# First mixer of a two-layer encoder step: index scores before the value product, forget gates before keys and queries, output-gate units between the level passes

## The reference, cut to what matters

```python
z = u @ w_in
aq, af, ai, ag, bq, bk, bv, bqi, bki, bw = jnp.split(z, split_at, axis=-1)
# gated linear recurrence (A), 4 heads of 128
qa = silu(aq);  ka = (1 - lb) * sigmoid(-af);  va = ai
log_f = logaddexp(log(lb), log1p(-lb) + log_sigmoid(af))     # forget gates
oa, s_fin = hgrn2_recurrence(qa, ka, va, log_f, s0)          # b = cumsum(log_f) in chunks of 64
oa = rms(oa) * o_gain * sigmoid(ag)                          # output gates
# sparse attention (B): index scores, the top keys of each row, then attention over them
q = rope(rms_norm(bq)); k = rope(rms_norm(bk)); qi = rope(bqi); ki = rope(bki)
score = sum_h relu(qi_h @ ki.T) * wi_h                       # wi = bw / 2
ob = attention(q, k, bv, top_k(score))
return concat(oa, ob) @ w_out
```

## Time and profile before

| | us |
|---|---|
| median of 3 runs | 2174.45 (2172.32 to 2175.32) |
| the profiled execution, its own time | 2178.14 |
| its span, first to last instruction | 2176.4 |
| PE busy | 1996.0 (92% of the span) |
| DVE / ACT / POOL busy | 1358.7 / 1111.3 / 778.2 |
| mean granted clock of PE | 0.957 of 2.4 GHz |

### The profile page before, as it was taken

How to read it: one execution, slowest core, us unless ns; L and a number is a source line. 1 busy time by engine, 2 the same in 40 slices (tenths; PEclk the granted TensorE clock), 3 DMA queues, 4 the chain that set the end, 5 groups by cost and what they waited for, 6 DMA issues and landing times. The chain is left out here.

```text
span 2176.4 us, 35434 instructions
## 1 busy us (share of the span) xinstructions
PE 1996.0 (92%) x13900; PEld 1508.1 (69%) x13900; DVE 1358.7 (62%) x2050; ACT 1111.3 (51%) x1334; POOL 778.2 (36%) x446
## 2 busy tenths in 40 slices
PE   4999999999998788979999997999999678999999
PEld 2677777665776655657777775777777456777777
DVE  7777853314987743276787437778743667778632
ACT  5677854112143234057778335777843217778621
POOL 4766500000037402147571014776400426667000
PEclk9999999997998889989999999999999879999999
DMA  3223222210111020012222211332322201322221
GB/s 134 85 93 113 92 100 80 87 49 5 63 59 63 6 87 20 20 39 97 97 97 100 107 66 39 108 104 97 101 99 73 79 3 60 115 97 92 99 105 40
DMA packets 24025, 167.06 MB, mean 77 GB/s; under 512 B 3024, under 2 KB 3024, under 8 KB 8176
## 3 DMA queue, kind: packets, MB, share of 16 engines
q1 hardware_dynamic: 22176, 157.98, 20.9%
q0 software_dynamic: 1744, 7.66, 1.0%
HBM read 161.80 MB, written 3.83 MB: 76 GB/s over the span
## 5 line engine op out<-in xcount | busy, mean ns | idle before, releaser
L1661 PE MATMUL ps<-big 128*128 128x296 f16 x2464 | 717.2, 291 | 39.6 <-ACT big L667 12.4
L1665 PE MATMUL ps<-big 128*128 128x296 f16 x2464 | 716.6, 291 | 13.1 <-DVE big L1013 12.8
L1662 PE MATMUL ps<-big 128*128 128x296 f16 x2464 | 716.9, 291 | 0.0
L1642 PE MATMUL ps<-big 128*128 128x296 f16 x4224 | 540.0, 291 | 10.5 <-DVE big L1113 10.4
L1642 PEld LDWEIGHTS ps<-big 128*128 128x128 f16 x4224 | 411.2, 98 | 133.4 <-DVE big L1113 11.7
L384 POOL TENSOR_TENSOR big<-big 128x512 f32<-128x512 f32 x88 | 123.4, 1402 | 634.5 <-ACT big L558 388.0
L1661 PEld LDWEIGHTS ps<-big 128*128 128x128 f16 x2464 | 242.1, 98 | 119.1 <-issue 16.1
L1665 PEld LDWEIGHTS ps<-big 128*128 128x128 f16 x2464 | 242.2, 98 | 91.1 <-DVE big L1013 20.9
L1636 PE MATMUL ps<-big 128*128 128x296 f32 x992 | 264.6, 429 | 34.3 <-DVE big L1571 25.3
L1662 PEld LDWEIGHTS ps<-big 128*128 128x128 f16 x2464 | 242.4, 98 | 67.7
L1636 PEld LDWEIGHTS ps<-big 128*128 128x128 f32 x992 | 195.2, 198 | 98.8 <-issue 25.4
(11 more groups left out here) (270 smaller groups left out, 2074.2 us busy)
## 6 DMA issues: line engine op xcount, KB each, us to landing
big<-in_w_up SPq DMA_DIRECT2D x88, 1024.0 KB, 4.8
big<-in_w_dn SPq DMA_DIRECT2D x32, 1408.0 KB, 6.0
big<-in_w_in SPq DMA_DIRECT2D x20, 512.0 KB, 3.5
big<-in_w_out SPq DMA_DIRECT2D x1, 4096.0 KB, 12.7
resid<-in_x SPq DMA_DIRECT2D x4, 592.0 KB, 6.6
out_y<-resid SPq DMA_DIRECT2D x8, 296.0 KB, 4.7
big<-in_w_ai POOLq DMA_DIRECT2D x1, 2048.0 KB, 10.1
big<-in_w_pool POOLq DMA_DIRECT2D x1, 1024.0 KB, 5.2
```

Of the source, the lines that this page charges most:

```text
L1642: last = mm(ps[:, bank + hf, 0:HALF], w, x[:, hf * HALF:(hf + 1) * HALF], start=start, stop=stop)
L1661: mm(out, w[:, 0, c], xop[:, 0, x, c], start=start, stop=False, skip_group_check=True)
L1662: mm(out, w[:, 1, c], xop[:, 0, x, c], start=False, stop=False, skip_group_check=True)
L1665: last = mm(out, w[:, 0, c], xop[:, 1, x, c], start=False, stop=(c == DC // 2 - 1), skip_group_check=True)
```

## The change

The units are put in another order, and so are the instructions of PE, ACT, DVE and POOL around them. In `w_in` the forget gates now come before the key: index key 0, index queries 1 and 2, `af` 3 to 6, key 7, queries 8 to 11, `aq` 12 to 15, `ag` 16 to 19. Core of the diff (lines that only move are mostly shown where they arrive):

```diff
+            pool.wait_ge(s["isc_acc"], 4 * TILES)
+            g.memset(att, 0.0).then_inc(s["att_zero"], 1)
+            pool.dma_start(states_hi[:, 2], d["state"]).then_inc(s["state_in"], 16)
             pool.wait_ge(s["gate_l1"], 1)
             link(g.tensor_scalar(gate_b, zf, 0.0, None, ALU.min))
...
+            def proj(n, dst, h, func):
+                act.wait_ge(unit_done, U + n + 1)
+                a.activation(split(dst[:, h]), halves(unit_bank(n)), func).then_inc(s["raw_evac"], 1)
+            for n, dst in enumerate((kit, qit[:, 0], qit[:, 1])):
+                act.wait_ge(unit_done, U + n + 1)
+                a.activation(split(dst), halves(unit_bank(n)), ACT.Copy).then_inc(s["raw_evac"], 1)
...
+            proj(AF, zf, 0, ACT.Copy)
+            for t in range(TILES):
+                act.wait_ge(s["ai_mm"], t + 1)
+                a.activation(va[0:ROWS[t], t], ps[0:ROWS[t], 4 + t % 2, :], ACT.Copy).then_inc(s["ai_evac"], 1)
+            for h in range(1, HEADS):
+                proj(AF + h, zf, h, ACT.Copy)
+            act.wait_ge(s["raw_evac"], 7)
...
+            def query(h):
+                act.wait_ge(unit_done, U + BQ + h + 1)
+                a.activation(split(qt[:, h]), halves(unit_bank(BQ + h)), ACT.Copy, scale=cgain[:, 0:1])
+                if h >= 1:
+                    act.wait_ge(s["ksum_mm" if h == 1 else "qsum_mm"], 1 if h == 1 else h - 1)
+                a.activation(split(square[:, (h + 1) % 2, :]), halves(unit_bank(BQ + h)), ACT.Square) \
+                    .then_inc(s["qk_sq"], 1)
+            proj(BK, kt.rearrange("p (h n) -> p h n", h=1), 0, ACT.Copy)
+            a.activation(split(square[:, 0, :]), halves(unit_bank(BK)), ACT.Square).then_inc(s["qk_sq"], 1)
+            query(0)
             act.wait_ge(s["ksum_mm"], 1)
             a.activation(split(root), halves(6), ACT.Sqrt, bias=eps[:, 0:1], scale=1.0 / DH) \
                 .then_inc(s["kroot_done"], 1)
-            for h in range(HEADS):
-                proj(12 + h, qa, h, ACT.Silu)
+            query(1)
...
-            for h in range(2):
-                proj(16 + h, ag, h, ACT.Sigmoid)
+            for h in range(2, HEADS):
+                query(h)
             for h in range(HEADS):
                 last = a.activation(ka[:, h], ka[:, h], ACT.Exp, bias=lb_ln[:, h:h + 1])
             last.then_inc(s["gate_ka"], 1)
-            for h in range(2, HEADS):
-                proj(16 + h, ag, h, ACT.Sigmoid)
+            act.wait_ge(s["qsum_mm"], 4)
+            a.activation(rqs[:, 0:4], ps[:, 4, 0:16].rearrange("p (t h) -> p t h", t=4), ACT.Sqrt, bias=eps[:, 0:1],
+                         scale=1.0 / DH)
+            a.activation(rqs[0:ROWS[4], 4], ps[0:ROWS[4], 4, 16:20], ACT.Sqrt, bias=eps[0:ROWS[4], 0:1],
+                         scale=1.0 / DH).then_inc(s["qroot_done"], 1)
+            for h in range(HEADS):
+                proj(AQ + h, qa, h, ACT.Silu)
             act.wait_ge(s["scan_done"], 1)
             diffs = 0
             for n, (kind, hp, h) in enumerate(DECAYS):
                 cols = NT if kind != "level" else MAIN if h == 64 else TAIL0 if h >= 16 else NT
                 e = decay[:, n % 2, :, 0:cols]
+                for h in range(HEADS):
+                    if n == GATE_AT[h]:
+                        proj(AG + h, ag, h, ACT.Copy)
...
+            act.wait_ge(s["raw_evac"], 16)
+            a.activation(ag, ag, ACT.Sigmoid).then_inc(s["ag_done"], 1)
...
+                a.activation(kd_tok[0:ROWS[t], t], ps[0:ROWS[t], t % 2, :], ACT.Copy).then_inc(s["kdt_evac"], 1)
...
+            dve.wait_ge(s["gate_logf"], 1)
+            for h in range(HEADS):
+                for lo, w in SEGMENTS:
+                    last = v.tensor_tensor_scan(zf[:, h, lo:lo + w], ones[:, 0:w], zf[:, h, lo:lo + w], 0.0, ALU.mult,
+                                                ALU.add)
+            last.then_inc(s["scan_done"], 1)
             dve.wait_ge(s["k_normed"], 1)
             dve.wait_ge(s["rope_in"], 32)
+            for n in range(5):
+                dve.wait_ge(s["kperm_mm"], n + 1)
+                rope(kt if n == 0 else qt[:, n - 1], 1, rope_bank(n))
+                dve.wait_ge(s["rope_done"], 3 + n + 1)
...
-            for n in range(5):
-                if n == 4:
-                    dve.wait_ge(s["gate_logf"], 1)
...
-            dve.wait_ge(s["raw_evac"], 16)
+            dve.wait_ge(s["raw_evac"], 12)
...
+                        ps[:, 2 + 3 * (n % 2) + pair, :].rearrange("p (a b n) -> p a b n", a=2, b=2))
...
+                        ps[0:r, 4 + 3 * (n % 2), 0:256].rearrange("p (b n) -> p b n", b=2)[:, :, 0:r])
...
+            dve.wait_ge(s["ag_done"], 1)
...
-                if 2 <= n < 8:
-                    pe.wait_ge(s["qk_sq" if 5 <= n else "raw_evac"], n - 4 if 5 <= n else n - 1 if n < 5 else 0)
+                if n >= 2:
+                    before = n - 1 if n > AG else n - 2
+                    if BK <= before < AQ:
+                        pe.wait_ge(s["qk_sq"], before - BK + 1)
+                    else:
+                        pe.wait_ge(s["raw_evac"], before + 1 if before < BK else before - 3)
                 w = wslot[:, n % 2, 0:DC * P].rearrange("p (c n) -> p c n", c=DC)
                 for c in range(DC):
                     if n == 0:
                         pe.wait_ge(normed_done, c + 1)
-                    last = product(2 * (n % 2), w[:, c, :], x[:, c, :], c, DC)
+                    last = product(unit_bank(n), w[:, c, :], x[:, c, :], c, DC)
...
+            def value_tile(t):
...
+            in_unit(0)
+            in_unit(1)
             pe.wait_ge(consts_in, 16 * 7)
-            for n, src in enumerate((kit, qit[:, 0], qit[:, 1])):
-                if n:
-                    in_unit(n)
-                    pe.wait_ge(s["raw_evac"], n)
-                    if n >= 2:
-                        pe.wait_ge(s["rope_done"], n - 1)
-                    exchange(0, (kit, qit[:, 0])[n - 1], 6, s["perm_mm"])
-            pe.wait_ge(s["ai_in"], 16)
+            pe.wait_ge(s["raw_evac"], 1)
+            exchange(0, kit, 6, s["perm_mm"])
+            in_unit(2)
+            pe.wait_ge(s["raw_evac"], 2)
+            pe.wait_ge(s["rope_done"], 1)
+            exchange(0, qit[:, 0], 6, s["perm_mm"])
+            pe.wait_ge(s["vw_in"], 16)
             for t in range(TILES):
-                pe.wait_ge(s["vw_evac"], TILES)
-                if t >= 2:
-                    pe.wait_ge(s["ai_evac"], t - 1)
-                for c in range(DC):
-                    last = mm(ps[0:ROWS[t], 4 + t % 2, :], x[:, c, cols(t)], w_ai[:, c, :], start=(c == 0),
-                              stop=(c == DC - 1))
-                last.then_inc(s["ai_mm"], 1)
-                if t == 0:
+                value_tile(t)
+                if t == 1:
                     pe.wait_ge(s["raw_evac"], 3)
                     pe.wait_ge(s["rope_done"], 2)
                     exchange(0, qit[:, 1], 6, s["perm_mm"])
...
-            pe.wait_ge(s["ai_evac"], TILES)
+            pe.wait_ge(s["vw_evac"], TILES)
...
+            in_unit(AF)
+            pe.wait_ge(s["ai_in"], 16)
+            pe.wait_ge(s["relu_done"], 4 * TILES)
+            for t in range(TILES):
+                if t >= 2:
+                    pe.wait_ge(s["ai_evac"], t - 1)
+                for c in range(DC):
+                    last = mm(ps[0:ROWS[t], 4 + t % 2, :], x[:, c, cols(t)], w_ai[:, c, :], start=(c == 0),
+                              stop=(c == DC - 1))
+                last.then_inc(s["ai_mm"], 1)
+            for n in range(AF + 1, BQ + 1):
                 in_unit(n)
-                pe.wait_ge(s["qk_sq"], n - 3)
-                pe.wait_ge(s["relu_done"], 4 * TILES)
-                if n == 4:
-                    product(6, ones[:], square[:, 0, :], 0, 1).then_inc(s["ksum_mm"], 1)
-                else:
-                    head_square_sums(mm, ps, square, ones, n - 5, s)
-            pe.wait_ge(s["qk_sq"], 5)
-            for n in range(8, IN_UNITS):
...
-                if n >= 15:
+            pe.wait_ge(s["qk_sq"], 1)
+            product(6, ones[:], square[:, 0, :], 0, 1).then_inc(s["ksum_mm"], 1)
+            pe.wait_ge(s["ai_evac"], TILES)
+            for h in range(HEADS):
+                in_unit(BQ + 1 + h)
+                pe.wait_ge(s["qk_sq"], h + 2)
+                head_square_sums(mm, ps, square, ones, h, s)
+            for n in range(5):
+                if n == 0:
                     pe.wait_ge(s["k_normed"], 1)
-                    if n > 15:
-                        pe.wait_ge(s["rope_done"], 3 + n - 15)
-                    exchange(1, kt if n == 15 else qt[:, n - 16], 6, s["kperm_mm"])
+                if n == 1:
+                    pe.wait_ge(s["qroot_done"], 1)
+                if n >= 2:
+                    pe.wait_ge(s["rope_done"], 3 + n - 1)
+                exchange(1, kt if n == 0 else qt[:, n - 1], rope_bank(n), s["kperm_mm"])
+                if n % 2 == 0 and n < 5:
```

(62 more changed lines are left out.)

27 lines of the change are left out of this document (1 added, 26 removed).

## The result

| | before | after |
|---|---|---|
| first comparison, median | 2174.89 us | 2156.7 us (2153.25 to 2158.66), ratio 0.9908 [0.9887, 0.9929] |
| comparison repeated later | 2174.03 us (17 runs) | 2157.39 us (2155.2 to 2161.05), ratio 0.9923 [0.991, 0.9936] |
| span of the profiled execution | 2176.4 us | 2155.0 us |

The change is worth 17 to 18 us, some 0.8%.

A forecast was written before the change was run, and what follows sets the result against it. Bound by PE, idle some 19 us at the level passes waiting for DVE's product. Passes ending 10.0 us earlier less 2.3 for the Sigmoid give 7.7: 2170.4 profiled, median 2166.7 us; range 2159.8 (and half a microsecond of spread) to 2174.5.

The forecast's parts named there:

- scores near 469: Index scores start without waiting for the `ai` product: at 469.2 instead of 503.5, ending at 496.5 instead of 530.8.
- gates near 620: Gate chain on ACT and POOL ends at 620.3; DVE, free at 609.4, waits 11 us for it.
- passes bound by PE: The main forecast for the level passes with four `ag` units among them; chance 0.68.
- series rival: Level passes: units stand in series with the loop, passes take 91.9 us, time 2181.2; chance 0.06.
- The passes with four units: 16 level passes plus four `ag` units: 77.5 us, ending at 731.7, 10.0 us earlier than before.
- The waits: PE waiting for DVE in the passes: 6 us, bounds 3 and 12.6.
- The cold start: First pass and unit 16, after 4.8 us of idle PE: 2.9 us extra.
- the passes' own work: PE's 16 level passes: 41.65 us busy at clock 0.88, so 36.7 warm.
- PE until the passes: PE's stretch up to the first level pass: last `aq` unit ends at 649.4, first pass at 654.2, 33.3 us earlier.
- The wait for the key's rope: Exchange of query 1, ahead of the passes: PE waits 1 us for the rope after the scan, bounds 0 and 5.
- Behind the passes: One Sigmoid ahead of the decayed keys' copies delays PE's third transpose by 2.3 us, bounds 1.0 and 3.
- the gain is eaten: Pass waits of 10 us or key's rope at 5: one leaves 3.7 us gain, both none; 2170.7 to 2174.7; chance 0.19.

The follow-up runs named there:

- the run with late scores: From the changed kernel, only the `ai` product moved back ahead of the index scores, units still in the passes; 2191.05 us, ratio 1.0075 to before.

## Why the prediction was wrong in its size

The mechanism was right point by point: scores near 469 (468.0), top-k and norm near 609 (606.4), gates near 620 (618.6), DVE idle before them (12.2 us), PE without a stop up to the last `aq` unit, passes bound by PE, waits for that product of DVE only (L1457, after the change L1458), a Sigmoid of 2.2 us ahead of the copies. The series rival did not happen. What was mis-sized, by the ledger above, against a gain of 17.4 us at the end of the passes where I had 10.0:

- **The passes with four units, 77.5 us forecast, 72.0 measured.** This is the step that failed. Three terms, all taken too high. The waits, 6 forecast, are 3.7 (0.71 + 0.98 + 0.68 + 0.39 + 0.98 and no more): I took "once or twice for each of the five stretches", and it was none in the first, twice in one and once in the others. DVE's first product instruction (L1456, after the change L1457) falls from 1079 to 935 ns in the mean; that POOL has finished more of its differences under the units would explain it, but is not shown. The cold start, 2.9 forecast, is 1.6: pass 0 takes 3.57 us instead of 2.0 and the unit behind it, at 8.14, is warm. I had priced it by a whole cold unit behind the scores, where the clock had been low for 30 us. And the passes' own work, 36.7 forecast, is 34.7 (68.3 busy, less 32 for the units and 1.6). I had multiplied the busy time by 0.88, but that clock is a mean over the whole window, idle time included. Stretches of 2 us of the kernel before, columns as in the earlier trace rows:

```profile
688.00:690.00 2.00, 2.00 (x12) 2.00 (x11) 1.77 (x2) 0.00 (x0) 2.00 (x2) 0.50 0.00 0
...
700.00:702.00 2.00, 0.00 (x0) 0.00 (x0) 2.00 (x2) 1.07 (x1) 0.90 (x1) 1.00 0.02 4
...
704.00:706.00 2.00, 2.00 (x12) 2.00 (x12) 1.30 (x3) 0.00 (x0) 2.00 (x1) 0.50 0.00 0
...
732.00:734.00 2.00, 2.00 (x12) 2.00 (x12) 0.96 (x3) 0.21 (x1) 2.00 (x2) 0.50 0.00 0
```

In the passes the clock stood at 0.50 for 5.7, 3.4 and 3.4 us (from 687.46, 703.39 and 730.70), and PE was busy through all 12.5 us of that, while its idle time lay at 1.00. Half of 12.5 off 41.65 is 35.4, not 36.7. The same stood in the earlier trace rows: a warm pair of passes took 4.42 us, and eight pairs are 35.4. The last 0.7 us lie at the eight joints of passes and units, where the records of the timeline overlap by some 0.16 us each.

- **PE until the passes, 33.3 us earlier forecast, 35.2 measured.** The wait for the key's rope (1 us) did not come: the scan ended at 624.9 and PE went on from 617.21 to 646.43 without a stop. Before also had a 0.47 us stop at another unit, which I left out; the last 0.4 us I can't place.
- **Behind the passes, 2.3 later forecast, 2.2 measured, and the clock gives 2.5 back.** The state products took 5.98 us instead of 8.43, which I had not considered. ACT's Sigmoid starts at 730.16, 0.02 us after its load of 1.28 us ends, and the load 0.02 us after the exponential ahead of it. The Trainium skill, "ScalarE: Activation LUTs", "What ACT_TABLE_LOAD costs", puts a drain of the engine beside each switch of tables; none shows here.
- The range took in waits of 3 us and no cold start, and so covered those two errors, but not the passes' own work nor the clock behind them. Those two terms, 4.5 us, are why 2156.7 fell outside, by 2.6.

The prediction also read the rows of before wrongly where it says that POOL's gates stretched one DVE instruction. There was a second, at the end of the top-k, with POOL's instruction beside it:

```profile
634.19 4.23 DVE L1385 TENSOR_SCALAR big<-big 80x528 f32<-80x528 f32 x1
```

```profile
632.90 5.23 POOL L438 TENSOR_TENSOR big<-big 128x2368 f32<-128x2368 f32 x1
```

In the changed kernel the same instruction takes 0.43 us, 3.8 less, and the norm's last step takes 2.1 more. So the norm ended 36.0 us earlier, counted from unit 0, and not 34.3. DVE waited for the gates behind it, so the time does not show it.

That DVE waits for POOL was one of the two ways to the rival "the gain is eaten" (0.19). It did not come where I looked for it: the key's rope took 2.4 us (624.80 to 627.18), not 5. It is real and large all the same, and at the end of the fourth tile it was missed by 0.6 us of time: in the run with late scores three instructions lost 10.6 us to it. The rule of the Trainium skill, "SBUF — State Buffer", "SBUF: two separate sides", that the loser waits for the whole instruction, agrees with the two longest rows (4.28 and 5.31 us, ending with POOL's).

## What to carry to other kernels

Where a loop over several engines leaves PE idle in small pieces, independent PE work between its turns costs only what it adds beyond those pieces: here 32 us of units lengthened the passes by 17.8. It pays only if that work was also the cover of nothing else, so ask what must come earlier for the loop to start without it (here the scores, the top-k, the gates and the scan: with late scores the same passes were a loss of 17 us). Price warm work from rows that ran warm, and not from busy time times the clock of a window that also holds idle time.

## What the runs showed of the hardware

- **Half clock behind the passes.** In the changed kernel the granted clock fell to 0.5 (1.2 GHz) some 3 us after the last pass and rose 10 us later, just ahead of the state products; with the first unit ahead of pass 0 it was low for 14 us, though PE did the same work with the same waits (4.28, 3.54 and 0.73 us) in both. The two versions with the Sigmoid behind the copies are a second such pair (4.28, 1.31 and 0.73 us): low for 14 us without the other edit and for 7 with it. Before, it was 14. The 48 state products took 8.43, 8.46, 8.55, 8.02 and 8.57 us in five profiles and 5.98 in six others, never less. What decides between the two is not shown: the same sequence gave both, so the moment at which it starts may count. It was not tried to shift it by a fixed delay.
- **POOL beside DVE.** DVE's L1389 (128x400) took 0.37 us alone and 4.28 beside a POOL instruction of 5.2 us, L1391 0.31 and 5.31; MAX8 and MATCH_REPLACE8 kept their 0.71 and 0.69 us beside such instructions.
- **Start of the stage.** Unit 0 started between 429.0 and 432.1 us in profiles whose code is the same up to there, and the rest of the program behind the mixer, the same code in all, spread by 6 us.
